# Merging two token mixers: the pooled half first, most of it in seven-product pairs, then the attention half

## The reference, cut to what matters

```python
merge = sigmoid(proj[..., o_merge:]).reshape(B, S, 2, D)          # gates, 1024 wide each
a = nsa_attention(...) @ w_attn_proj                              # (S,512) @ (512,1024)
b = pool_mixer(...)    @ w_pool_proj                              # (S,512) @ (512,1024)
x = x + (merge[..., 0, :] * a + merge[..., 1, :] * b) @ w_out     # output projection
```

## Time and profile before

| | |
|---|---|
| time, median of 3 runs (lowest to highest) | 1386.22 us (1385.82 to 1386.26) |
| span of the profiled execution, first to last instruction | 1385.2 us |
| TensorE busy | 1374.7 us, 99% |
| VectorE busy | 1039.6 us, 75% |
| ScalarE busy | 739.7 us, 53% |
| GpSimd busy | 207.9 us, 15% |
| merge stage, from its first pooled product to the first output product | 569.85 to 663.66 us |

### The profile page before, as it was taken

One profiled execution on the slowest core, in us unless ns is written; L12 is line 12 of the kernel. 1 busy time (PEld: TensorE's weight loads), 2 busy tenths in 40 slices (PEclk: granted clock), 3 DMA queues, 4 the chain that ended last, 5 costly groups with the idle time before them and its releaser, 6 DMA issues.

```text
span 1385.2 us, 19117 instructions
## 1 busy us (share of the span) xinstructions
PE 1374.7 (99%) x6581; PEld 1138.1 (82%) x6581; DVE 1039.6 (75%) x2050; ACT 739.7 (53%) x1437; POOL 207.9 (15%) x203
## 2 busy tenths in 40 slices
PE   9999999999999999999999999999999999999998
PEld 7788778888888888788888888888888888888887
DVE  6977487888788878856568877778695968777764
ACT  6433446666666666522235655545454645555464
POOL 5233100101010100000230030212213040302100
PEclk9999999999999999999999999999999999999999
DMA  7446531222222121754232184654738192846553
GB/s 223 123 152 178 160 91 54 65 62 65 60 68 61 48 68 47 236 182 151 76 94 89 47 146 97 129 107 85 136 82 162 49 157 69 150 94 122 106 168 122
DMA packets 162141, 151.75 MB, mean 110 GB/s; under 512 B 12691, under 2 KB 125127, under 8 KB 162048
## 3 DMA queue, kind: packets, MB, share of 16 engines
q1 hardware_dynamic: 145920, 121.20, 28.9%
q0 software_dynamic: 16128, 29.37, 14.4%
HBM read 94.43 MB, written 56.10 MB: 109 GB/s over the span
## 4 chain that ended last, share of the span: by engine, by line
PE 96%; DVE 1%; ACT 1%; DMA 1%; issue 1%; POOL 0%; ACTq 0%; POOLq 0%; DVEq 0%
PE psU L2282 5%; PE psU L2283 5%; PE psU L2284 5%; PE psX L2552 5%; PE psU L2735 4%; PE psU L2737 4%; PE psU L2736 4%; PE psX L2282 4%; PE psX L2283 4%; PE psX L2284 4%; PE psU L2772 4%; PE psU L2774 4%; PE psU L2773 4%; PE psX L2735 3%; PE psX L2737 3%; PE psX L2736 3%
## 5 line engine op out<-in xcount | busy, mean ns | idle before, releaser
L1038 POOL DMA_DIRECT2D residual_scratch<-csum x112 | 98.3, 915 | 483.0 <-DVE csum L2166 415.7
L1989 DVE TENSOR_TENSOR ring_lo<-raw,ring_hi 128x512 fp32r<-128x512 f32 x150 | 103.0, 686 | 62.6 <-ACT ring_hi L1334 62.4
L1334 ACT ACTIVATE ring_hi<-raw 128x512 fp32r<-128x512 f32 x150 | 92.6, 624 | 64.0 <-PE psU L2774 23.3
L1221 ACT ACTIVATE pth<-psX 128x512 fp32r<-128x512 f32 x148 | 88.1, 595 | 71.8 <-PE psX L2552 71.1
L1887 DVE TENSOR_TENSOR ptl<-psX,pth 128x512 fp32r<-128x512 f32 x132 | 90.4, 688 | 25.5 <-ACT pth L1221 23.9
L1213 ACT ACTIVATE prob<-prob,nb 128x640 f32<-128x640 f32 (+7 forms) x128 | 93.4, 730 | 25.3 <-DVE nb L1861 25.2
L2282 PE MATMUL psX<-ahi,whi 128*128 128x512 f32 x256 | 103.3, 403 | 0.1
L2283 PE MATMUL psX<-alo,whi 128*128 128x512 f32 x256 | 100.9, 394 | 0.0
L2284 PE MATMUL psX<-ahi,wlo 128*128 128x512 f32 x256 | 100.5, 393 | 0.0
L2552 PE MATMUL psX<-ident,prob 128*128 128x128 f32 x592 | 89.5, 273 | 0.3 <-DVE ptl L1887 0.2
L1010 POOL TENSOR_TENSOR wlo<-wraw,whi 128x1024 fp32r<-128x1024 f32 x14 | 33.6, 2402 | 329.6 <-DVE prob L1875 329.6
(11 more groups left out here) (377 smaller groups left out, 4043.5 us busy)
## 6 DMA issues: line engine op xcount, KB each, us to landing
raw<-in_w_ff_dram SPq DMA_DIRECT2D x120, 256.0 KB, 4.3
residual_scratch<-csum POOLq DMA_DIRECT2D x112, 256.0 KB, 5.9
wraw<-in_w_in_dram SPq DMA_DIRECT2D x21, 512.0 KB, 4.1
gate_scratch<-zst SPq DMA_DIRECT2D x32, 256.0 KB, 3.8
mg<-gate_scratch SPq DMA_DIRECT2D x16, 512.0 KB, 3.4
proj_scratch<-stage SPq DMA_DIRECT2D x30, 256.0 KB, 2.0
duo_w<-in_w_in_dram SPq DMA_DIRECT2D x20, 256.0 KB, 4.6
xt<-in_x_dram SPq DMA_DIRECT2D x8, 512.0 KB, 7.9
```

The costliest lines, as they stand in the source:

```text
L1038: pool.dma_start(resid[rows, cols], sums[b][e][:], accum_op=ALU.add).then_inc(added[b][e], 16)
L1334: nc.scalar.activation(weights_of(g)[0], raw_of(g), ACT.Copy).then_inc(w_hi, 1)
L1989: nc.vector.tensor_tensor(lo, raw_of(g), hi.bitcast(f32), ALU.subtract).then_inc(w_lo, 1)
```

## The change

The merge stage is split in two phases.

**Pooled phase.** Blocks 0 and 1 are computed plainly (48 matmuls, one weight load of 256 columns). Blocks 2 to 7 form three pairs (`MIX_DUOS`), each a 2x2 problem of two output blocks by two token halves, contraction 512 in 2x2 blocks, done in seven products of 6 matmuls each. The combined token operands S1 to S4 (`mix`, each 2 tiles of 128x512) are built once: GpSimd computes the eight raw tiles from `yraw` (`mix_rawly`), ScalarE and VectorE split them (`mix_token_hi`, `mix_token_lo`). The weight combinations are made by VectorE (`mix_combine`), and the weights are split in pieces of 128x256 in a ring of eight (`mix_hi`, `mix_lo`), five products ahead. Results are copied or added into `branch` (`copy_mix`, `take_pooled` on ScalarE; `sum_mix`, `take_pooled` on VectorE). GpSimd adds 1 to each pooled gate in `mg` (`one_more`, 128x1024) and multiplies it into `branch` in place (`gate_pooled`, four 128x512 for each two blocks). The transposes of x stand behind products 1 and 4 of each pair.

**Attention phase.** Eight blocks of 24 matmuls; VectorE applies one gate from PSUM (`z0`), adds `branch`, and writes `alo` as before.

The matmuls of the stage go from 384 to 366. The number of seven-product sets before the MLP (`ALL_DUOS`) shifts some semaphore counts. The hardware loops of the stage are written out. The per-buffer semaphores of x rows and of the output stores are merged into one set (`row_io`).

```diff
@@ tiles
-        mg = place("mg", [P, 2, 2, HALF])
+        mg = place("mg", [P, 2, S])
+        branch = at("branch", [P, KT, S], ALO)
+        mix_ring = [(at(f"mix_hi{c}", [P, 2, P], WHI + TILE // 2 * c, f32r), at(f"mix_lo{c}", [P, 2, P], WLO + TILE // 2 * c, f32r))
+                    for c in range(8)]
@@ sync
             for h in range(2):
                 store_z(2 * KT - 1, h)
-            load_ab(N3 + 2, N3 % 2, 2)
             load_x(2, False, 0)
-            load_ab(N3 + 3, (N3 + 1) % 2, 3)
-            load_gates(1, False)
+            load_pool_gate(0)
+            load_mix(N3 + 2, (N3 + 2) % 2)
+            load_x(3, False, 1)
+            load_pool_gate(1)
...
@@ gpsimd
+            pool.wait_ge(misc_ev, N_MISC)
+            pool.wait_ge(u_done, 2 * N3)
+            for name, j in MIX_RAW:
+                mix_rawly(name, j)
...
+            one_more(0)
+            one_more(1)
+            for m in range(2):
+                for h in range(2):
+                    gate_pooled(m, h)
+            for m in range(2, KT, 2):
+                one_more(m)
+                one_more(m + 1)
+                for side, h in ((0, 0), (1, 1), (1, 0), (0, 1)):
+                    gate_pooled(m + side, h)
@@ scalar
             part_hi(ohi[:, 0:2], oraw[0][:])
-            split_hi(N3 + 1, (N3 + 1) % 2, raw_need(N3 + 1))
+            def mix_hi(c):
...
+                if c == 0:
+                    for h in range(2):
+                        act.wait_ge(st_z[h], 16 * 2 * KT)
...
+            mix_hi(0)
+            mix_hi(1)
+            mix_hi(2)
+            for name, j in MIX_OPS[0:4]:
+                mix_token_hi(name, j)
+            take_pooled(0)
+            mix_hi(3)
             act.wait_ge(o_in[1], 16)
             act.wait_ge(o_in[2], 16)
             for h in range(2):
                 part_hi(ohi[:, 2:4, h * HALF:(h + 1) * HALF], oraw[1][:, :, h * HALF:(h + 1) * HALF])
+            take_pooled(1)
+            for name, j in MIX_OPS[4:8]:
+                mix_token_hi(name, j)
+            mix_hi(4)
+            act.wait_ge(yo_lo, 4)
+            keep_x(0)
+            keep_x(1)
@@ vector
+            mix_lo(0)
+            mix_combine(0)
+            mix_lo(1)
+            mix_combine(1)
             dve.wait_ge(xr_t, 2)
             part_lo(olo[:, 0:2], oraw[0][:], ohi[:, 0:2], 5)
-            split_lo(N3 + 1, (N3 + 1) % 2)
+            mix_lo(2)
+            mix_combine(2)
+            for name, j in MIX_OPS[0:4]:
+                mix_token_lo(name, j)
+            mix_lo(3)
+            mix_combine(3)
             dve.wait_ge(yo_lo, 4)
             for h in range(2):
                 cols = slice(h * HALF, (h + 1) * HALF)
                 part_lo(olo[:, 2:4, cols], oraw[1][:, :, cols], ohi[:, 2:4, cols], h + 6)
+            take_pooled(0)
+            for name, j in MIX_OPS[4:8]:
+                mix_token_lo(name, j)
+            take_pooled(1)
+            mix_lo(4)
+            keep_x(0)
+            keep_x(1)
@@ tensor
+            def mix_product(p, i):
...
+                if i == 0 and p == 0:
+                    pe.wait_ge(ev[1], N1 + 1)
...
+                elif i == I_B21:
+                    pe.wait_ge(*((summed, 3 * (q - 1) + 1) if p else (ev[1], N1 + 2)))
...
-            for m in range(2):
-                mixers(N3 + m, (N3 + m) % 2, m, m, m)
-            with pe.Fori(1, KT // 2) as j:
-                for u in range(2):
-                    mixers(N3 + u + 2 * j, (N3 + u) % 2, 2 * j + u, u, None)
+            pe.wait_ge(w_lo, N3 + 1)
+            for h in range(2):
+                pe.wait_ge(yo_lo, h + 2)
+                for m in range(2):
+                    pool_part(h, m)
+            for p in range(MIX_DUOS):
+                for i in range(N_PROD):
+                    mix_product(p, i)
+                    if i in (I_B21, I_T3):
+                        turn_next(2 + 2 * p + (i == I_T3))
+            for m in range(KT):
+                attention_part(m)
```

More of the change, by code:

```diff
@@ L391, in hybrid_trunk @@
         fin_last = sem("fin_last")
[L392 removed]
         def raw_need(n):
[L396 to L397 removed]
+            return 16 * (n // 2 + 1)
         def proj_col(n):
@@ L2658, in pool_part, with attention_part @@
+            def attention_part(m):
+                n, u = N3 + KT // 2 + m // 2, m % 2
+                pe.wait_ge(w_lo, n + 1)
+                for h in range(2):
+                    if m == 0:
+                        pe.wait_ge(d_last, ALL_DUOS - 1 + h)
+                    elif m == 1:
+                        pe.wait_ge(summed, 3 * ALL_DUOS)
+                    else:
+                        pe.wait_ge(ab_read, 2 * m + h - 3)
                     for k in range(4):
-                        three(psU[:, 2 * h + 1], slot, k, 4 + k, yhi, ylo, slice(h * HALF, (h + 1) * HALF), k == 0, k == 3)
@@ L2661, in attention_part @@
-                def attention_part(h):
-                    for k in range(4):
-                        if peeled == 0 and k % 2 == 0:
+                        if m == 0 and k % 2 == 0:
                             pe.wait_ge(yo_lo, 4 if k == 0 else 5 + h)
-                        last = three(psU[:, 2 * h], slot, k, k, ohi, olo, slice(h * HALF, (h + 1) * HALF), k == 0, k == 3)
+                        last = three(psU[:, 2 * u + h], n % 2, k, 2 * k + u, ohi, olo, slice(h * HALF, (h + 1) * HALF), k == 0, k == 3)
```

389 lines of the change are left out of this document (287 added, 102 removed).

## The result

| | before | after |
|---|---|---|
| time, median (lowest to highest) | 1386.16 us (1385.82 to 1386.26), 4 runs | 1400.27 us (1399.91 to 1400.78), 4 runs |
| ratio of the times, 95% interval | | 1.0102 (1.0088 to 1.0115) |
| profiled execution: time, span | 1386.2, 1385.2 us | 1399.9, 1397.9 us |
| first pooled product, first output product | 569.85, 663.66 us | 569.57, 677.27 us |

The change costs 14.1 us. In the profiled executions the merge stage takes 107.7 us for 93.8, 13.9 more. The stages before it take 0.3 us less and those behind it 0.9 less (720.6 for 721.5), so the span grows by 12.7; the time outside the span is 2.0 us after and 1.0 before. The loss is in the merge stage.

A forecast was written before the change was run, and what follows sets the result against it. The prediction took TensorE, busy 1374.7 of 1385.2 us, to bound the kernel. Its terms, -4.1 - 1.1 + 9.0 + 2.9 + 1.6 = +8.3 us, gave 1394.5 us, range 1387.5 to 1399.5.

The forecast's parts named there:

- Removed work: Merge stage on TensorE: 384 matmuls become 366, saving 4.1 us, and a 1.1 us wait for olo goes too.
- the old wait: TensorE's wait for VectorE's olo near the merge stage's start, ended at 577.88; its 1.1 us was forecast to go.
- First wait: Before the first product: TensorE stands from 580.7 to 589.7 for VectorE's first copy, 9.0 us (bounds 4.2 to 12.7).
- The fifteen instructions: VectorE's queue ahead of its first copy out of PSUM; rival A would need them done in 8.6 us from 572.1.
- Second wait: Before the second product: TensorE waits for VectorE's second copy behind four lo parts, 2.9 us (1.7 to 4.1).
- Clock: Behind the two waits: TensorE restarts at half the pace, adding 1.6 us (0 to 3.2).
- Pairs at 0: Rest of the pooled phase: VectorE's 7.0 us a pair is covered by TensorE's 11.6, costing 0.
- rival C: In the pairs: GpSimd's gate products make VectorE the bound, could cost 1 us a pair, 1397.5 us; chance 0.15.
- Transfers at 0: SyncE's queue at the start: last gate stores landed by 573.4 are early enough to be hidden by the GpSimd chain.
- Attention phase at 0: Attention blocks: TensorE takes 5.4 us a block, VectorE's six instructions 4.1, so cost 0.
- the 1.0 us between span and time: Whole kernel: median time 1386.2 is 1.0 us above the span of 1385.2, taken as unchanged.
- Rival A: Merge stage start: copies are out by 580.7 and only the removed matmuls count, 1381.0 us, faster; chance 0.05.

The follow-up runs named there:

- experiment 9: Changed kernel in its own order with all of GpSimd's new work replaced by memsets that read nothing; 1387.85 us, ratio 1.0015.
- experiment 1: Changed kernel with GpSimd's one_more of blocks 0 and 1 held until VectorE's second copy out of PSUM; 1399.35 us, ratio 1.0097.
- experiment 11: Changed kernel with engine and load queues reordered, gating on VectorE, and both engines' copies out of pooled banks placed when their bank is done; 1387.63 us, ratio 1.0015.
- Experiment 3: Changed kernel with 40 extra matmuls of unused result in TensorE's first wait; 1399.42 us, ratio 1.0097.
- experiment 5: Changed kernel with raw tiles by memset of 0 and one_more only behind VectorE's second copy; 1393.73 us, ratio 1.0045.
- 6: Changed kernel with VectorE and ScalarE queues reordered: first olo in VectorE's idle time, copies in front, one_more late, nothing left out; 1393.76 us, ratio 1.0058.
- 12: Kernel of experiment 11 with ScalarE's copy of the first product's bank early and VectorE's fourth-product lo parts ahead of the row copy; 1387.76 us, ratio 1.0012.

## Why the prediction was wrong in size, step by step

**Removed work: right.** 18 matmuls and the old wait are gone (-5.2 us), and the stage ends with the transposes and products that were counted.

**First wait: the failed step, 9.0 forecast, 12.3 measured.** The prediction led the path to the first copy over GpSimd's last raw tile, at 583.3, and let VectorE go on from there by itself, 6.6 us "back to back". Both halves failed. GpSimd ended at 581.4, and VectorE did not wait for it at all: its last idle time ended at 574.46, with the gate stores, and from there it worked through its queue. That the part behind the first `olo` began at 583.43, as forecast, was luck: four pieces of 128x256 had taken 1.5 us each, and `olo` 3.37. Up to there VectorE took 9.0 us for what takes 3.6 in experiment 9, so 5.4 us are the raw tiles' company. From there on it was not alone either: 8.8 us up to the copy for 6.0 in experiment 9, of which 0.8 are the first lo part (1.25 for 0.41), 0.85 the four lo parts and 1.06 the two halves of `olo`. These 2.7 us are most of the 3.3 that the term lacked. The mis-sized term is `one_more`, which the prediction priced at 1.2 us each by an affine_select row and let meet nobody. It takes 4.1 beside VectorE and 2.8 even with little beside it (607.51), and experiment 1 shows that it is this that stretches the chain: 9.5 us without it. The other 4.1 us of the wait stand in experiment 9 too: VectorE's own instructions, 10.2 us up to the end of the copy (574.41 to 584.67), that begin behind the gate stores.

The Trainium skill has a rule for such meetings (SBUF — State Buffer, Who interferes with whom): a VectorE instruction with two SBUF inputs contends with a GpSimd instruction that reads SBUF, not with one that only writes, and what they share is an exclusive lock. The rows agree on who meets: 128x256 pieces take 1.5 us beside GpSimd instructions of 1.35, the copies out of PSUM (no second SBUF input) keep their 0.68 to 0.69 us (577.94 in experiment 11, inside a raw tile), and memsets cost VectorE nothing (experiment 9). They do not show that one waits for the whole of the other. Beside a raw tile a piece loses 1.1 us, most of the tile's length and as much as the larger lo part of the earlier trace rows. But `one_more` takes 2.8 us and held VectorE for 0.8 to 1.1 at a time, and a piece with two SBUF inputs took its lone 0.41 us inside it (594.75 in experiment 1). What decides this no run shows.

**Second wait: 2.9 forecast, 2.3 measured**, within its bounds. The four lo parts took 4.64 us and the copy 0.6, near the upper price of 5.5.

**Clock: 1.6 forecast, 3.1 measured**, at the upper bound of 3.2. Twelve matmuls at 0.43 for 0.23 us are 2.4, the transposes 0.7. The two waits follow each other so closely that the granted clock stays at 0.50 from 588 to 600. The Trainium skill's sentence that an idle array falls to 1.2 GHz (TensorE: Matmul & The Clock Gate, What's actually happening) holds here, by the 0.50 of those rows. Experiment 3 shows how little of it could be had back: 0.9 us between the medians, with overlapping executions.

**Pairs at 0: nearly right for this kernel** (0.46 us at 620.73, in the second pair, where the prediction said that a wait would prove it wrong). With a shorter first wait the pairs wait 3.9 us beside GpSimd's gating (experiment 1), rival C's mechanism; in experiment 5 it is 3.5, and with the gating by memset and the same first wait nothing (experiment 9). Taken one by one the terms are not independent.

**Transfers at 0: wrong.** The prediction named 573.4 as early enough for the gate stores, "hidden by the GpSimd chain". ScalarE began its first weights behind them at 574.01, and there was no GpSimd chain to hide it: VectorE stood for 2.58 us and then had no gap up to the copy. By an estimate from these rows up to 2.6 us of the first wait are due to it. No run has the stores earlier; the experiments from 6 on, except 9, put the first `olo` into the gap instead, so that it is no longer idle.

**Attention phase at 0: right**, no wait of TensorE after 621 us in the stage.

Sum of what was measured: -4.1 - 1.1 + 12.3 + 2.3 + 3.1 + 0.5 = 13.0, against 13.9 for the length of the stage (107.70 for 93.81). The rest was not traced singly; part of it is that the first matmul behind a wait is followed 0.57 us later (593.02 to 593.59), not 0.43. One more term was taken as unchanged and was not: the 1.0 us between span and time is 2.0 in the execution profiled after. Most of that is no cost of the change, since the executions of the kernel before that ran beside the experiments have 1.7 to 1.9.

**Rival A was wrong by its own point**: no copy was out by 580.7, and even with all of GpSimd's company gone it comes at 583.99 (experiment 9). The fifteen instructions take VectorE 10.2 us alone, more than the 8.6 that the prediction gave them. Only with the copies moved (11) does TensorE pass 580.4 without a wait, and then it waits later.

No version tried is faster than the kernel before. The best that computes the whole layer (11, and 12 with it) takes 1.7 us more than the kernel before and 12.6 less than the kernel after; it keeps the seven-product pairs but not the gating on GpSimd.

## What to carry to other kernels

An engine that looks idle is no free place for elementwise work if its reads hold up the busy one: GpSimd's work cost 12.4 us here. Ask of each instruction how many SBUF inputs it and its neighbours have, and take the price from a row in which such a pair meets: 0.42 us became 1.5 beside tiles of 1.3. Where TensorE is at 99%, moving work in front of its first product has to be summed engine by engine up to that product, from the moment at which each engine can start; an average of a third free over the stage says nothing of the first 20 us. And if a shorter wait brings a new one a product or two later, stop moving instructions: then it is the time that the busy engine's work takes that binds, its meetings included.

## What the runs showed that was not expected

- One-input GpSimd work is not cheap. `tensor_scalar` 128x1024 takes 2.8 us where VectorE is mostly elsewhere (607.51) and 4.1 beside it (581.33), and ScalarE adds the 1 in 1.05. A two-input subtraction of the same shape takes GpSimd 2.4 us elsewhere in the kernel (third line below), and VectorE needs 1.2 us for two inputs of this shape. The Trainium skill (GPSIMD Engine Reference, 4.1 Engine selection) calls one input roughly line-rate for GpSimd; the 2.8 us do not agree with that.
- GpSimd's memset of 128x512 takes 0.5 us and leaves VectorE alone, so it serves to switch off the meeting with every instruction in its place; it is shorter than what it replaces, and that is switched off with it.
- The sixteen gate products as VectorE's scalar_tensor_tensor take 0.68 us each, with the addition included; on GpSimd the same work took 25.4 us of `one_more` and 24.2 us of products.

GpSimd's groups in the kernel after (busy us and mean ns of one, idle before):

```profile
L1126 POOL TENSOR_SCALAR mg<-mg 128x1024 f32<-128x1024 f32 x8 | 25.4, 3186 | 15.4 <-DMA mg<-gate_scratch 15.4
L1121 POOL TENSOR_TENSOR branch<-mg,branch 128x512 f32<-128x512 f32 x16 | 24.2, 1535 | 3.7 <-DVE branch L2162 3.7
...
L1083 POOL TENSOR_TENSOR wlo<-wraw,whi 128x1024 fp32r<-128x1024 f32 x14 | 33.6, 2402 | 329.7 <-DVE prob L2064 329.7
```
